# A two-layer transformer block on one core: mixers' ends in another order, a halved last pair, and alpha x added by TensorE

## The reference

```python
for layer in range(DEPTH):
    h = _swa_nsa_mixer(...) if layer % 2 == 0 else _mla_mixer(...)
    x = _layer_norm(DEEPNORM_ALPHA * x + h, ln_mix_g[layer], ln_mix_b[layer])
    f = _moe(x, ...)        # sum over 6 of 64 experts of w * (silu(x @ Wg) * (x @ Wu)) @ Wd, plus a shared expert
    x = _layer_norm(DEEPNORM_ALPHA * x + f, ln_ffn_g[layer], ln_ffn_b[layer])
```

## Time and profile before

| what | value |
|---|---|
| median of 3 runs | 1278.81 us |
| profiled execution, its own time | 1280.48 us |
| its span on the core | 1278.4 us |
| PE busy | 1187.5 us (93%) |
| DVE / ACT busy | 367.8 us (29%) / 257.0 us (20%) |
| mean DMA rate over the span | 348 GB/s |
| first to last instruction of L852, layer 0 and 1 | 189.8 us to 1252.8 us |

### The profile page before, as it was taken

One profiled execution on the slowest core, in us unless ns is written; L12 is line 12 of the kernel. 1 busy time (PEld: TensorE's weight loads), 2 busy tenths in 40 slices (PEclk: granted clock), 3 DMA queues, 4 the chain that ended last, 5 costly groups with the idle time before them and its releaser, 6 DMA issues.

```text
span 1278.4 us, 20339 instructions
## 1 busy us (share of the span) xinstructions
PE 1187.5 (93%) x8235; PEld 673.9 (53%) x8235; DVE 367.8 (29%) x746; ACT 257.0 (20%) x546; POOL 16.0 (1%) x22
## 2 busy tenths in 40 slices
PE   7998899999999998989869989999999999999984
PEld 4554465555556554646435645564646655454541
DVE  0575561212122121212142456221212212121213
ACT  1232421111112111111104532211211111111110
POOL 0000000000000000000000000000000000000000
PEclk9998999999999999999979999999999999999997
DMA  9535249999999999999991535799999999999993
GB/s 346 150 130 233 107 199 377 418 419 419 419 419 419 420 421 420 421 420 419 420 387 41 197 149 223 322 418 420 418 419 417 419 420 420 421 420 421 419 420 140
DMA packets 67754, 444.55 MB, mean 348 GB/s; under 512 B 7664, under 2 KB 12144, under 8 KB 16368
## 3 DMA queue, kind: packets, MB, share of 16 engines
q1 hardware_dynamic: 67696, 443.71, 85.1%
HBM read 442.63 MB, written 1.05 MB: 347 GB/s over the span
## 4 chain that ended last, share of the span: by engine, by line
PE 61%; DMA 31%; DVE 3%; issue 2%; ACT 1%; POOL 1%; SPq 0%; POOLq 0%; DVEq 0%
DMA ring<-in_expert_w_up 31%; PE psum L852 22%; PE psum L875 9%; PE psum L971 5%; PE psum L800 3%; PE psum L902 3%; PE psum L692 3%; PE psum L584 2%; PE psum L1112 2%; PE psum L728 2%; PE psum L706 1%; PE psum L637 1%; PE psum L627 1%; PE psum L759 1%; PE psum L886 1%
## 5 line engine op out<-in xcount | busy, mean ns | idle before, releaser
L852 PE MATMUL psum<-ring,arena 128*64 128x256 f32 x4032 | 458.8, 380 | 33.6 <-DMA ring<-in_expert_w_up 21.3
L852 PEld LDWEIGHTS psum<-ring,arena 128*64 128x64 f32 x4032 | 297.7, 137 | 211.7 <-DMA ring<-in_expert_w_up 31.3
L875 PE MATMUL psum<-ring,room 128*64 128x512 f32 x1008 | 233.8, 598 | 1.9 <-issue 1.0
L1808 DVE TENSOR_TENSOR y_low<-psum,y_high 128x1024 fp32r<-128x1024 f32 x64 | 78.4, 1225 | 366.6 <-ACT y_high L1276 366.6
L875 PEld LDWEIGHTS psum<-ring,room 128*64 128x64 f32 x1008 | 69.5, 136 | 133.5 <-issue 112.6
L1799 DVE SCALAR_TENSOR_TENSOR room<-room,arena,psum 128x256 f32<-128x256 f32 x64 | 30.7, 480 | 347.8 <-PE psum L852 347.8
L1276 ACT CAST y_high<-psum 128x1024 fp32r<-128x1024 f32 x64 | 64.8, 1013 | 250.9 <-PE psum L875 250.9
L1290 ACT COPY room<-psum 128x256 f32<-128x256 f32 x64 | 23.9, 373 | 262.9 <-PE psum L886 262.9
L902 PE MATMUL psum<-y_high,spread 32*128 32x512 f32 x512 | 65.5, 501 | 5.0 <-issue 4.9
L800 PE MATMUL psum<-onehot,x_high 128*128 128x256 f32 x256 | 66.0, 298 | 0.0
L800 PE MATMUL psum<-onehot,x_low 128*128 128x256 f32 x256 | 63.0, 283 | 0.0
(11 more groups left out here) (237 smaller groups left out, 875.0 us busy)
## 6 DMA issues: line engine op xcount, KB each, us to landing
ring<-in_expert_w_gate SPq DMA_DIRECT2D x126, 1024.0 KB, 18.7
ring<-in_expert_w_up SPq DMA_DIRECT2D x126, 1024.0 KB, 19.7
ring<-in_expert_w_down SPq DMA_DIRECT2D x126, 1024.0 KB, 18.0
ring<-in_swa_nsa_w_in SPq DMA_DIRECT2D x8, 1036.0 KB, 14.0
room<-in_swa_nsa_w_out SPq DMA_DIRECT2D x2, 2048.0 KB, 7.9
room<-in_mla_w_out SPq DMA_DIRECT2D x1, 4096.0 KB, 23.2
ring<-in_mla_w_in SPq DMA_DIRECT2D x1, 2688.0 KB, 19.7
ring<-in_mla_w_uq SPq DMA_DIRECT2D x1, 2304.0 KB, 12.5
```

Of the source, the lines that this page charges most:

```text
L852: mm = pe.matmul(BANK[2 + m][CAP * e:CAP * e + CAP, 0:DE], xg[:, c, 2 * j + e, :], expert(stored[e])[0][:, c, m, :], start=c == 0, stop=c ...
L875: mm = pe.matmul(PS[0][CAP * e:CAP * e + CAP, half * 512:(half + 1) * 512], ht[:, c, CAP * e:CAP * e + CAP], expert(stored[e])[1][:, c, ha ...
L1808: V.tensor_tensor(ylo, PS[0][:, :], yhi.bitcast(F32), ALU.subtract).then_inc(sem[f"yd_dve{L}"], 1)
```

## The change

- **Layer 0, ACT:** the copy of the compressed probabilities (cpt) stands ahead of the exponentials of unit 8 instead of behind them.
- **Ends of the mixers:** `mixed` is cut in two. The sums of tc 0 are taken earlier: in layer 0 both ahead of the last `nsa_columns`, in layer 1 around the last `normalise`; there the LayerNorm of tc 0 stands ahead of the last `heads_out`. `x_low` of tc 0 moves behind the LayerNorm of tc 1. On PE both column halves of tc 1 stand ahead of the turning of tc 0. In layer 1 tc 1 accumulates in PS[1] instead of PS[3], all 16 matmuls of tc 0 stand ahead of the turning of unit 6, and 8 of the 16 of tc 1 (those that need only the earlier heads) stand ahead of the values of units 6 and 7.
- **alpha x:** DVE makes `alpha_ident` = ALPHA times the identity once per layer. In the first group, pair 2, behind its gate and up, PE adds alpha x to ACC with 4 float32 matmuls of 128x512 (`pe_residual`). The pass of L1599 is gone; bn_stats and the first step of `normed` read ACC in PSUM.
- **Last pair:** its high and low parts are taken by column halves (`y_high_tail`, `y_low_tail`), the first once the first half of `pe_down` is done (`tail_pe`), and `pe_combine_tail` adds them with 8 matmuls over all 128 rows, half 0 and then half 1, instead of 16 over 32 rows.

```diff
+        def pe_residual(pe, tc):
+            for half in range(2):
+                pe.matmul(ACC[tc][:, half * 512:(half + 1) * 512], alpha_ident,
+                          xrow[:, tc, half * 512:(half + 1) * 512], start=False, stop=False)
...
+                if last and j == GP - 1 and not half:
+                    mm.then_inc(sem["tail_pe"], 1)
...
+        def pe_combine_tail(pe, L, p, half):
+            pe.wait_ge(sem["tailhi_act"], 2 * L + half + 1)
+            pe.wait_ge(sem["taillo_dve"], 2 * L + half + 1)
+            pe.wait_ge(sem[f"spread_dve{L}"], p + 1)
+            cols = slice(half * 512, (half + 1) * 512)
+            for tc in range(TC):
+                for part in (yhi, ylo):
+                    mm = pe.matmul(ACC[tc][:, cols], spread[:, 1, tc * P:(tc + 1) * P], part[:, cols],
+                                   start=False, stop=part is ylo)
+                if half or tc == TC - 1:
+                    mm.then_inc(sem["acc_pe"], 1)
...
                     pe_gate_up(pe, L, i, j, beyond)
+                    if shared_step(i, j, 0):
+                        pe.wait_ge(sem["alpha_dve"], L + 1)
+                        for tc in range(TC):
+                            pe_residual(pe, tc)
...
             n = OUT_STEPS[L]
-            pe_out_part(pe, L, 1, range(n))
+            pe_out_part(pe, L, 1, range(n - 4, n))
+            pe_out_part(pe, L, 1, range(2 * n - 4, 2 * n))
             pe_columns(pe, st, 0, "lnmix_dve", TC * L)
-            pe_out_part(pe, L, 1, range(n, 2 * n))
...
+            def y_high_tail(p):
+                act.wait_ge(sem[f"comb_pe{L}"], p)
+                act.wait_ge(sem["tail_pe"], L + 1)
+                nc.scalar.copy(yhi[:, 0:512], BANK[0]).then_inc(sem["tailhi_act"], 1)
+                act.wait_ge(sem[f"down_pe{L}"], (p + 1) * 2)
+                nc.scalar.copy(yhi[:, 512:D], BANK[1]).then_inc(sem["tailhi_act"], 1)
...
-            act_exp(act, 0, 8)
             act.wait_ge(sem["cpt_pe"], 1)
             nc.scalar.copy(cpt, v(BANK[3], u=4, q=P)).then_inc(sem["cpt_act"], 1)
+            act_exp(act, 0, 8)
...
+                src = r if part == "mix" else ACC[tc][:, :]
...
-                    dve.wait_ge(sem["acc_pe"], L * TC + tc + 1)
-                    r = xrow[:, tc, :]
-                    link(V.scalar_tensor_tensor(r, r, ALPHA, ACC[tc][:, :], ALU.mult, ALU.add))
-                    V.bn_stats(stats[:, 0:6], r[:, 0:512])
-                    link(V.bn_stats(stats[:, 6:12], r[:, 512:1024]))
+                    for half in range(2):
+                        dve.wait_ge(sem["acc_pe"], L * BOTH["acc_pe"] + 1 + (1 + tc) * half)
+                        link(V.bn_stats(stats[:, 6 * half:6 * half + 6], ACC[tc][:, half * 512:(half + 1) * 512]))
                     normed(tc, "ffn")
```

## The result

| | before | after |
|---|---|---|
| median of the timed runs | 1278.57 us (4 runs, 1278.12 to 1281.76) | 1257.94 us (4 runs, 1256.17 to 1258.57) |
| profiled execution | 1280.48 us | 1257.87 us |
| its span | 1278.4 us | 1255.9 us |

The ratio is 0.9831, with a 95% interval of 0.9812 to 0.985: the kernel got 20.6 us faster. The forecast was 1256.5 us in 1250 to 1264. The profiled executions differ by 22.6 us, where the terms had 22.4; the medians differ by 2 us less. All timed runs of the kernel before together spread from 1276.6 to 1282.3 us, and experiment 3 shows what they differ by.

The account below looks back on a forecast made before the run. The prediction took the expert stream to bound each mixture, so only time ahead of the first refill and behind the last expert counts. Terms of -22.4 us took 1280.48 to 1258.1, less 1.7 for the median: 1256.5 us, range 1250 to 1264.

Parts of the forecast that it names:

- A: Layer 0's compressed turn: copy ahead of exponentials saves 2.0 us of PE idling and 1.4 of half clock, -3.4 us.
- B: Layer 0's mixer end: tc 1's matmuls run together, second logits start at 167.15 instead of 171.31 us, -4.2 us.
- C: Layer 1's mixer end: eight tc 1 matmuls fill PE's idle time, second logits at 781.15 instead of 785.25, -4.1 us.
- D, layer 1: Behind the last mixture: split last pair and shorter LayerNorm end at 1269.5 instead of 1275.35 us, -5.8 us.
- D, layer 0: Behind layer 0's mixture: -4.2 us to the end of tc 0's LayerNorm, -0.7 from clock, together -4.9 us.
- E: Alpha x on PE in the first group's pair 2: 3.5 us per layer, stream still fed, 0 us.
- Later the slack grows: Refills after the twelfth issue: PE frees twelve issues in 50.6 us where the stream needs 60.
- Rival 1: In the mixtures, the stream pauses for alpha x, 1 to 3.5 us per layer: 1258.5 to 1263.5 us; chance 0.10.
- Sum: Whole kernel: terms total -22.4 us, taking the profiled execution from 1280.48 to 1258.1 us.
- the subtraction of 1.7 us: Step from profiled execution to median of runs, taken as 1.7 us lower: 1258.1 becomes 1256.5 us.
- Rival 2: Full clock does not come back at the mixer's turn and end (1.4, 1.6) nor behind the mixture (0.7): 1260; chance 0.10.
- Rivals 3 and 4: Late weights for pairs 0 and 1 hide mixer gains: 1268, chance 0.05; delayed second logits bring half clock: 1293, chance 0.03.

Follow-up runs that it names:

- experiment 3: Changed kernel with 24 or 12 extra PE turnings, or 24 plus 8 with alpha x moved: 1254.02, 1256.63, 1250.12 us; repeated unedited 1258.04 us.
- root_alone: Changed kernel with DVE waiting for POOL's inverse root ahead of the first LayerNorm pass of both mixers: 1257.7 us.
- undo_mix: Changed kernel with both mixers' ends as before (order of output matmuls, sums, x_low and banks of tc 1): 1264.5 us.
- after_again: The changed kernel once more, without edits, timed and profiled again: 1258.04 us.
- alpha_last: Changed kernel with alpha x added in the first pair of the last group instead of pair 2 of the first: 1255.58 us.

## Why the prediction was right

The forecast, its range and its sign held. Step by step:

- **A**, -3.4: the idle time went from 2.68 to 0.72 and the eight pieces from 5.16 to 3.70, -3.4; undone, it cost 3.6.
- **B**, -4.2, and with A -7.6 to the first gate product: measured -8.0, of which 0.6 were there ahead of A (108.68 against 109.25). Undone, 3.8. DVE was 0.98 us late, inside the 0.5 to 1 that was said.
- **C**, -4.1: 4.3 when undone.
- **D, layer 1**, -5.8: measured -6.7, beyond the bound of -6.3. This term was mis-sized. The step was "the rest (3.35 ...) is as before": it counted DVE's instructions right and took over the 0.51 us in which DVE waits for POOL, twice. The first pass now reads PSUM, POOL's root took 0.55 instead of 1.52 us, and the wait is gone: 1.0 us. The Trainium skill, "SBUF — State Buffer" (Who interferes with whom), says that a DVE instruction with two SBUF inputs contends with a GpSimd instruction that reads SBUF, and that one with at most one SBUF input, outside the 2-port modes, doesn't. The trace agrees, with 1.52 and 0.55 us, and root_alone shows that it is the pass beside it.
- **D, layer 0**, -4.9: the -0.7 of clock didn't come. The 3.33 us were paid like the 6.52 in the profiled execution (10.16 us for the projection, before 9.61), which agrees with what the Trainium skill, "TensorE: Matmul & The Clock Gate" (Part 1, HAM oscillation), says of idle gaps, as quoted in the prediction. The rest was -4.5 for -4.2 (14.14 to 9.64 us from the last down product to the first turning).
- **E**, 0: it was 0 in layer 0 and +0.6 to +0.8 us in layer 1. The step that failed is "Later the slack grows". It holds for whole groups, but in group 2 the shared chunks' down product (7.1 us) and the round that refills one expert use up the lead again (2.0 us left in the kernel before, by the estimate above), so that the stream pauses for 0.9 us. Rival 1 was the right mechanism at the wrong place, below its lower bound of 1 us a layer.
- **Sum**: -22.4 against -22.5 in the profiled executions. So close a sum is partly luck: D in layer 1 gained 0.9 us more than its term, and E with 0.6 and the clock in layer 0 with 0.7, and 0.5 more for the longer projection, gained less than theirs, which nearly cancels. The 1.4 us by which the median missed is in the subtraction of 1.7 us: the profiled execution of before was above the middle of its runs, that of after was not.

Rival 2 holds for D alone: in A and B the clock stayed full. Rivals 3 and 4 fall: undo_mix paid B and C in full, and the wait ahead of the second logits stayed under 1 us at full clock.

## What to carry to other kernels

Where PE's lead over a stream hides new work, follow the lead to its lowest point in the whole loop, special rounds included, and not only to the first place behind the edit. When an operand moves from SBUF to PSUM, look at who works beside that instruction. And where PE waits and then works on the critical path, a few matmuls whose result nobody reads can be worth more than a shorter wait: here 32 turnings and the move of alpha x gave 7.9 us of 1258, about 7 of them at the two places of the turnings (3.4 and 3.8 us, the profiled execution against after's).

## What the hardware showed unexpectedly

- One small instruction of POOL takes 0.55 us or 1.52 us, by whether DVE's pass beside it reads two operands from SBUF (1.45 to 1.53 us in all eight cases of before) or one from PSUM.
- Behind a wait of 1.08 us among small products TensorE went from 2.4 to 1.2 GHz, and it did not once the wait was filled; behind waits of 1.10 us among large ones it did not, and behind 2.03 us it did. Behind the same wait and with the same code it stayed at the lower clock for some 3.5, 7 or 10 us (after_again, alpha_last, after). With this, runs of one kernel differ by up to 5 us.
